# Expert mixture behind three attention layers: order of the last two experts, the last down product by column halves, the router's product with its columns held, the first weight remainders on GpSimd

## The reference

```python
def expert_choice_moe(h, w_router, w_gate, w_up, w_down):
    cap = CAPACITY_FACTOR * S // N_EXPERTS                    # 128
    aff = softmax(einsum('bsd,de->bse', h, w_router), axis=-1)
    g, idx = lax.top_k(aff.transpose(0, 2, 1), cap)
    xin = hb[ib]                                              # gather, for each expert
    a = einsum('becd,edf->becf', xin, w_gate)
    u = einsum('becd,edf->becf', xin, w_up)
    y = einsum('becf,efd->becd', silu(a) * u, w_down)
    y = y * g[..., None]
    return zeros((S, D)).at[ib].add(y)                        # scatter-add

    h2 = rmsnorm(x, norm_ffn_g) * (1.0 + sc2) + sh2           # in the block
    x = x + g2 * expert_choice_moe(h2, w_router, w_gate, w_up, w_down)
```

## Time and profile before

| | us |
|---|---|
| median of 3 runs | 2714.86 (2714.76 to 2715.02) |
| the profiled execution, timed | 2715.4 |
| its span | 2713.6 |
| window attention | 1836 to 2063 |
| router stage | 2063 to 2112.5 |
| experts | 2112.5 to 2713.6 |

### The profile page before, as it was taken

How to read it: one execution, slowest core, us unless ns; L and a number is a source line. 1 busy time by engine, 2 the same in 40 slices (tenths; PEclk the granted TensorE clock), 3 DMA queues, 4 the chain that set the end, 5 groups by cost and what they waited for, 6 DMA issues and landing times. The chain is left out here.

```text
span 2713.6 us, 32074 instructions
## 1 busy us (share of the span) xinstructions
PE 2501.0 (92%) x11641; PEld 1627.9 (60%) x11641; DVE 1729.4 (64%) x3267; ACT 1253.3 (46%) x2017; POOL 505.4 (19%) x525
## 2 busy tenths in 40 slices
PE   7999999699998899989999997999994699999997
PEld 3344444354555886446556656885552588888886
DVE  2799999677764421325654436506556688888885
ACT  2221110254554266345455542244444477777773
POOL 0000001011110000008677640000220011111111
PEclk9999999899999899999999997998996799999999
DMA  3011831211010332045343224030014799999994
GB/s 132 8 62 38 75 93 39 89 40 48 24 46 17 134 94 68 12 145 159 112 120 110 82 78 142 4 126 32 32 47 170 280 377 385 388 383 387 391 388 158
DMA packets 123818, 374.19 MB, mean 138 GB/s; under 512 B 22552, under 2 KB 31464, under 8 KB 122128
## 3 DMA queue, kind: packets, MB, share of 16 engines
q1 hardware_dynamic: 106064, 312.34, 31.3%
q0 software_dynamic: 17600, 59.81, 9.6%
HBM read 327.00 MB, written 45.11 MB: 137 GB/s over the span
## 5 line engine op out<-in xcount | busy, mean ns | idle before, releaser
L513 PE MATMUL ps<-l_hT,l_w 128*128 128x512 f32 (+1 forms) x832 | 364.3, 597 | 2.6 <-DVE l_hT L242 2.6
L513 PEld LDWEIGHTS ps<-l_hT,l_w 128*128 128x128 f32 (+1 forms) x832 | 155.3, 189 | 204.3 <-issue 204.2
L964 ACT ACTIVATE a_pT<-ps 128x512 f32<-128x512 f32 (+3 forms) x368 | 164.1, 487 | 173.6 <-PE ps L850 172.8
L894 PE MATMUL ps<-l_wo,a_mixT 128*128 128x512 f32 x384 | 182.1, 602 | 3.3 <-ACT l_klT L988 1.1
L1505 DVE MAX8 l_best<-sel 128x8 f32<-128x384 f32 (+5 forms) x192 | 171.6, 894 | 5.4
L976 ACT ACTIVATE a_p<-ps,a_stat 128x384 f32<-128x384 f32 (+7 forms) x192 | 129.2, 673 | 88.8 <-DVE a_stat L1050 49.9
L1506 DVE MATCH_REPLACE8 sel<-l_best,sel 128x384 f32<-128x384 f32 (+5 forms) x192 | 168.1, 876 | 0.0
L976 ACT ACTIVATE l_lat<-ps,a_stat 128x1024 f32<-128x1024 f32 (+7 forms) x128 | 94.8, 741 | 150.0 <-DVE a_stat L1050 149.1
L835 PE MATMUL ps<-l_kT,l_raw 96*128 96x512 f32 (+3 forms) x384 | 147.3, 492 | 5.7 <-ACT l_lat L976 4.1
L850 PE MATMUL ps<-ident,a_p 128*128 128x128 f32 x608 | 97.9, 290 | 30.8 <-DVE a_p L1063 27.5
L2737 POOL DMA_INDIRECT out_dram<-m_q,e_token x16 | 39.6, 2478 | 463.1 <-DVE m_q L2905 463.1
(11 more groups left out here) (460 smaller groups left out, 5712.5 us busy)
## 6 DMA issues: line engine op xcount, KB each, us to landing
x_raw<-in_w_gate SPq DMA_DIRECT2D x25, 2048.0 KB, 11.1
x_raw<-in_w_up SPq DMA_DIRECT2D x24, 2048.0 KB, 11.4
x_raw<-in_w_down SPq DMA_DIRECT2D x23, 2048.0 KB, 10.1
ada_w<-in_w_ada POOLq DMA_DIRECT2D x64, 384.0 KB, 3.7
m_ufT<-in_w_down SPq DMA_DIRECT2D x9, 2048.0 KB, 12.0
m_ufT<-in_w_up SPq DMA_DIRECT2D x8, 2048.0 KB, 11.7
l_w<-in_e_w_in SPq DMA_DIRECT2D x7, 2048.0 KB, 8.5
m_ufT<-in_w_gate SPq DMA_DIRECT2D x7, 2048.0 KB, 9.9
```

Source lines behind the costliest of these rows:

```text
L513: last = nc.tensor.matmul(self.t.ps[0:m, bank, :], w[:, c, col * P:col * P + m], hT[:, c, half * 512:(half + 1) * 512], start=c == 0, stop ...
L894: last = nc.tensor.matmul(t.ps[:, 7, :], self.lhs_out(n, self.order[n], c), self.w_out[:, c, h * 512:(h + 1) * 512], start=c == 0, stop=c ...
L964: self.k.nc.scalar.activation(dst, src, ACT.Copy).then_inc(self.moved["act"], 1)
```

## The change

Four edits.

1. In the window attention the router's columns become the stationary operand: `wg` is widened to 32 columns, of which 16 are zero, and chunk `c` of a block goes to the column group `c % 4`, that is to 32 rows of PSUM. ACT copies the four partial sums (`r_part`), and one more matmul with a matrix `pick` of ones adds them and turns them back, at the first pair of the next block (`sum_parts`). Blocks 6 and 7 are done as before.
2. The remainders of the first three halves are made on GpSimd in the router stage, between its stores and its gather, instead of on DVE at the start of the experts.
3. At the end up(15) runs ahead of down(14); the loads, ACT's and DVE's lists follow, h(15) is transposed within down(14) and goes to the buffer of `x_T0`.
4. Down(15) is made in column halves: 24 matmuls for columns 0 to 511, then 24 for the others. Each half has its own scaling and its own indirect DMA, with row numbers `halves` for an output seen as 2048 rows of 512.

```diff
+        elif b >= 0 and u % at.per == self.TURN + 1:
+            x = at.turns[u, "part"]
+            old = at.in_order[x.n - 2]
+            e.wait_ge(at.moved[old.engine], old.moved)
+            e.wait_ge(at.moved["act"], at.turns[u - 1, "row", 1].moved)
+            for i in range(2):
+                for g in range(4):
+                    c = 4 * i + g
+                    last = self.nc.tensor.matmul(self.t.ps[32 * g:32 * g + 32, x.bank, 0:P], self.wg[:, c, :], self.rT[b % 2][:, c, :],
+                                                 start=i == 0, stop=i == 1)
+            last.then_inc(at.turned, 1)
+
+    def sum_parts(self, e, at, b):
+        col = self.COL + EXPERTS * self.place(b)
+        e.wait_ge(at.moved["act"], at.turns[at.per * (b + 2) + self.TURN + 1, "part"].moved)
+        self.nc.tensor.matmul(self.t.ps[:, 6, col:col + EXPERTS], self.parts[b % 2][:], self.pick[:], start=True, stop=True).then_inc(self.routed, 1)
 
     def pe_beside(self, e, at, u):
 
-        b = u // at.per - 2
-        if b >= 0 and u % at.per == self.TURN + 1:
-            e.wait_ge(at.moved["act"], at.turns[u - 1, "row", 1].moved)
-            self.logits(b, range(KD))
+        b = u // at.per - 3
+        if b >= 0 and u % at.per == 0:
+            self.sum_parts(e, at, b)
...
         if m == self.UP:
-            return 6 * x + 2
+            return 6 * x + 2 if x + 1 < EXPERTS else 6 * x
...
-        return 6 * x + 6 if x + 1 < EXPERTS else 6 * x + 4
+        return 6 * x + {EXPERTS - 2: 8, EXPERTS - 1: 4}.get(x, 6)
...
+            for n in range(weights.SLOTS):
+                weights.low(e, n, nc.gpsimd)
             e.wait_ge(x_out, 16 * NB)
             e.wait_ge(told, 1)
             gather(0)
...
-            e.wait_ge(scattered, 16 * EXPERTS)
+            e.wait_ge(placed, 3)
+            for i in range(2):
+                e.wait_ge(yready, EXPERTS + i)
+                e.wait_ge(scattered, 16 * LAST)
+                nc.gpsimd.indirect_dma_start(t.out.rearrange("s (i d) -> (s i) d", i=2), bass.IndirectOffsetOnAxis(ap=halves[:, i:i + 1], axis=0),
+                                             last_y[:, 512 * i:512 * i + 512], None, compute_op=ALU.add).then_inc(scattered, 16)
+            e.wait_ge(scattered, 16 * (EXPERTS + 1))
...
+            for x in range(LAST):
+                up(x)
+                gate(x + 1, x)
+                if x == LAST - 1:
+                    up(LAST)
+                down(x)
+            last_down()
...
-            weights.low(e, 0)
-            weights.low(e, 1)
             e.wait_ge(xturn, 2)
...
-            for n in range(2, 5):
+            for n in range(SLOTS, 5):
                 weights.low(e, n)
```

More of the change, by code:

```diff
@@ L790, in __init__ @@
                     n += 1
+            elif rows and u >= 2 * self.per and u % self.per == rows.TURN + 1:
+                moved["act"] += 1
+                before = [x.used for x in self.turns.values() if x.n == n - 4]
+                self.turns[u, "part"] = Turn(n, "act", moved["act"], None, before[0])
+                n += 1
             ready += pair.joined
@@ L1174, in __init__ @@
         self.nc, self.t, self.a, self.gain, self.y = k.nc, t, a, gain, y
-        self.wr, self.wg = k.sb("r_w", [P, KD, EXPERTS]), k.sb("r_wg", [P, KD, EXPERTS])
+        self.wr, self.wg = k.sb("r_w", [P, KD, EXPERTS]), k.sb("r_wg", [P, KD, 32])
+        self.parts = [k.sb(f"r_part{i}", [P, P]) for i in range(2)]
+        self.pick = k.sb("r_pick", [P, EXPERTS])
         self.shift = k.sb("r_shift", [P, KD, P])
@@ L1268, in act @@
             if b >= 2:
-                e.wait_ge(self.routed, b - 1)
+                e.wait_ge(at.turned, at.turns[u - 2 * at.per + 1, "part"].n + 1)
             for i in range(2):
@@ L1274, in act @@
             self.square(e, b).then_inc(self.squared, 1)
+        elif b >= 0 and u % at.per == self.TURN + 1:
+            x = at.turns[u, "part"]
+            e.wait_ge(at.turned, x.n + 1)
+            if b >= 2:
+                e.wait_ge(self.routed, b - 1)
+            self.nc.scalar.activation(self.parts[b % 2][:], self.t.ps[:, x.bank, 0:P], ACT.Copy).then_inc(at.moved["act"], 1)
     def act_end(self, e, at):
-        e.wait_ge(self.routed, NB - 3)
+        e.wait_ge(at.turned, at.turns[len(at.pairs) - 1, "part"].n + 1)
         for i in range(2):
@@ L2564, in high, with low @@
                                       self.raw[n % self.RAWS].rearrange("p k n -> p (k n)"), ACT.Copy).then_inc(self.high_made, 1)
-    def low(self, e, n):
+    def low(self, e, n, engine=None):
         if n < self.N:
@@ L2570, in low @@
             high, rest = (x[:].rearrange("p k n -> p (k n)") for x in self.w[i])
-            self.nc.vector.tensor_tensor(rest, self.raw[n % self.RAWS].rearrange("p k n -> p (k n)"), high.bitcast(F32),
-                                         ALU.subtract).then_inc(self.split, 1)
+            (engine or self.nc.vector).tensor_tensor(rest, self.raw[n % self.RAWS].rearrange("p k n -> p (k n)"), high.bitcast(F32),
+                                                     ALU.subtract).then_inc(self.split, 1)
 def router_stage(k, a, t, keep, at, gate_w, token, weights, gather):
@@ L2728, in _ @@
         def _(e):
-            for x in range(EXPERTS):
+            for x in range(LAST):
                 for n in (1, 2) if x == 0 else (x + 2,):
@@ L2784, in gate, with up @@
                         chunk(x, xT[x % 2], GATE, 0, i, c)
-            turn_x(0)
-            gate(0)
-            for x in range(EXPERTS):
+            def up(x):
                 if x:
@@ L2796, in _, with down @@
                         turn_x(1)
-                if x < LAST:
-                    gate(x + 1, x)
-                else:
-                    turn_h(x)
+            def down(x):
                 if x:
@@ L2809, in _, with last_down @@
                         turn_x(x + 2)
+                        if x == LAST - 1:
+                            turn_h(LAST)
+            def last_down():
+                n = weights.at(LAST, DOWN)
+                e.wait_ge(silu, LAST + 1)
+                for half in range(2):
+                    cols = slice(half * 512, (half + 1) * 512)
+                    for i in range(2):
+                        e.wait_ge(w_split, n + i + 1)
+                        e.wait_ge(hsplit, 2 * LAST + i + 1)
+                        high, low = w[(n + i) % SLOTS]
+                        for c in range(HK):
+                            for j, (l, r) in enumerate(((last_hT[0], high), (last_hT[0], low), (last_hT[1], high))):
+                                last = nc.tensor.matmul(ps[:, half, :], l[:, i * HK + c, :], r[:, c, cols],
+                                                        start=i + c + j == 0, stop=i == 1 and c == HK - 1 and j == 2)
+                    last.then_inc(last_made, 1)
+            turn_x(0)
+            gate(0)
+            for x in range(LAST):
+                up(x)
+                gate(x + 1, x)
+                if x == LAST - 1:
+                    up(LAST)
+                down(x)
+            last_down()
         @block.scalar
@@ L2844, in _, with high_h @@
             first_of_h(0)
-            for x in range(EXPERTS):
+            def high_h(x, dst):
+                for i in range(2):
+                    e.wait_ge(hturn, 2 * x + i + 1)
+                    nc.scalar.activation(flat(dst[0][:, 4 * i:4 * i + 4, :]), ps[:, 2 + i, :], ACT.Copy).then_inc(hhigh, 1)
+            for x in range(LAST):
                 weights.high(e, 6 * x + 5)
@@ L2849, in _ @@
                 weights.high(e, 6 * x + 6)
-                for i in range(2):
-                    e.wait_ge(hturn, 2 * x + i + 1)
-                    if x:
-                        e.wait_ge(w_used, done(x - 1, DOWN))
-                    nc.scalar.activation(flat(hT[0][:, 4 * i:4 * i + 4, :]), ps[:, 2 + i, :], ACT.Copy).then_inc(hhigh, 1)
+                if x:
+                    e.wait_ge(w_used, done(x - 1, DOWN))
+                high_h(x, hT)
                 weights.high(e, 6 * x + 7)
@@ L2860, in _ @@
                 weights.high(e, 6 * x + 10)
+            high_h(LAST, last_hT)
+            weights.high(e, weights.N - 1)
         @block.vector
@@ L2881, in _, with result_h @@
                                         ALU.subtract).then_inc(xready, 1)
-            for n in range(2, 5):
+            for n in range(SLOTS, 5):
                 weights.low(e, n)
-            for x in range(EXPERTS):
-                weights.low(e, 6 * x + 5)
-                if x == 0:
-                    low_x(1)
+            def result_h(x):
                 e.wait_ge(silu, x + 1)
@@ L2890, in _, with low_h @@
                 nc.vector.tensor_tensor(h[:], h[:], ps[:, 2:4, :].rearrange("p a n -> p (a n)"), ALU.mult).then_inc(hready, 1)
-                weights.low(e, 6 * x + 6)
+            def low_h(x, dst):
                 for i in range(2):
```

50 lines of the change are left out of this document (41 added, 9 removed).

## The result

| | us |
|---|---|
| before, median of 6 runs | 2714.94 (2711.55 to 2717.71) |
| after, median of 6 runs | 2696.3 (2692.78 to 2698.82) |
| ratio | 0.9929, 95% interval 0.9917 to 0.9942 |
| forecast | 2696.4, range 2692.5 to 2705.5 |
| the profiled execution of after, timed / span | 2692.78 / 2691.0 |

The change takes 18.6 us off. The profiled execution of after is the fastest of its six, so the two spans are 22.6 us apart, 4 more than the medians. Stretches of the two traces are therefore compared from one event to another, never by their place in the span.

What follows compares the result with a forecast made beforehand. It took PE to bound the window attention and middle experts, DVE's subtractions the experts' start, and PE's waits and scatters the end. Gains 4 + 6.5 + 8 = 18.5 us gave 2696.4 against the median, range 2692.5 to 2705.5.

Steps and rivals of the forecast that it cites:

- Part 1: Window attention: router's columns stationary in four column groups, blocks 0 to 5, 4 us less, bounds +1.9 and -6.3.
- the columns do not overlap: Rival in window attention: the router product in column groups costs 1.9 us instead of giving 4, 2702.3; chance 8%.
- Part 2: Start of the experts: first three remainders on GpSimd, gate(0) starts at 2116.7 instead of 2123.26, 6.5 us less.
- given back: Rival at the experts' start: late transfers or slower GpSimd leave 0 instead of 6.5 us, 2702.9; chance 12%.
- Part 3: Experts' end: up(15) ahead of down(14), last down and scatter in column halves, 8 us less, bounds -3.6 and -9.
- The port: Slower rival in the router stage: DVE's top-k locks out with GpSimd's subtractions, up to 26.4 us, 2722.8; chance 7%.

Runs made afterwards that it cites:

- run 1: Before with only the router edit (columns stationary in four column groups, plus a summing product): 2709.8 us, 0.998 against before.
- Run 5: After, with all eight router products of a block summed in one column group instead of four: 2704.1 us.
- run 7: After, with 20 unused matmuls added to keep PE busy ahead of gate(0): 2695.9 us in a single run.
- run 2: Before with only the first three remainders moved to GpSimd: 2706.6 us, 0.9962 against before.
- run 3: Before with only the experts' end changed (up(15) ahead of down(14), last down by column halves): 2707.6 us, 0.9969 against before.
- run 4: After, with the last down whole again, in the old order with one scatter of 1024 columns: 2694.3 us, 0.9926 against before.
- Run 8: After, with one small unused DVE add, both inputs in SBUF, in each of the 16 top-k rounds: 2721.3 us.
- run 9: After, last down by weight halves, expert 14 scaled before the last remainder, which awaits scatter 14's issue and is made in two column halves: 2693.7 us.

## Why the prediction was right

**Part 1, -4.** Right in kind, and undersized. The four-group record was the one term without a row; I assumed 0.05 us, it is 0.036, nearly the 0.028 of a full overlap. The sum of the parts costs 0.14 a block and not 0.21. Per block 0.99 instead of 0.7, in all 5.9 by the rows, 5.8 by the stretch of the two profiles, 5.1 by the medians of run 1. The waits that I costed at nothing were 0.3 us once. Run 5 shows the rival "the columns do not overlap" as it would have been: 2704.1 for my 2702.3.

The Trainium skill (TensorEngine Tiling (Array Packing), Theoretical Speedup) has up to 4x for this shape; the runs show 1.87 / 0.57 = 3.3 between one group and four, the switch back to the full array within the 0.57.

**Part 2, -6.5.** Right term by term: 8.85 us apiece for the 8.8 taken from the earlier trace rows, the last over at 2096.2 with 3.9 us to the gather, gate(0) 2.1 us behind the transposes' end, the 3.2 us wait for `x_T1l` still there. The landings had 0.7 and 1.2 us of slack for the 0.5 and 1.0 forecast, so the rival "given back" was about as near as I thought. What I left out is PE's clock behind its idle stretch: gate(0)'s 48 matmuls took between 12.8 and 13.8 us in the traces of ten kernels (before, after and all but run 7), in no order that the edits explain. So one profile tells the gain no better than to a microsecond or so. Up to the transposes of h(0) it is 6.9 us between before and after, 6.4 between before and run 2; the other 1.1 us of the 8.0 in the table lie in the steady part behind (493.2 us in before and in run 2, 492.0 in after), which the change does not touch.

**Part 3, -8.** 7.1 in the stretch. PE ends 6.3 us earlier relative to the multiplication of h(14), for 6.2 forecast; its wait is 0.7 and not 1.2. Scatter 14 landed in 6.10 us, as summed. The term that was missized is what follows: between that landing and the next issue I had nothing, the chain shows 0.78 us (2679.99 to 2680.77), so the last scatter is issued 1.5 us behind PE's end and not 1.0. And the half scatter's end: 8.4 us from its issue to the span's end for my 5.0 + 3.0 = 8.0. Together 0.9 us, the whole difference between forecast and this profile; but the stretch of the same end varies by 1.0 us (run 3), so only the 0.78 us is sure, which stands between landing and issue in all six kernels whose last scatters wait for scatter 14 (0.77 to 0.78). The range from issue to the span's end is 7.9 to 8.4 us for the last half scatter, and the 8.0 that I summed lies in it. One thing that I counted as a gain is none, the column halves: the shorter vector instruction and the shorter landing stood in the sum with 0.6 and 1.1 us, and run 4 has the same time without them.

**The port.** Against it I had only one row of another instruction (L1027 in the earlier trace rows) and gave 7%. Run 8 bears out both halves: an instruction that meets the lock waits for the rest of GpSimd's, and the top-k's instructions don't meet it.

**The sum.** 4 + 6.5 + 8 = 18.5 stood for 18.6 by the medians; the stretches say 5.8 + 6.6 + 7.1 = 19.5. The errors of parts 1 and 3, +1.8 and -0.9, cancelled by half, and the medians are uncertain by some 3 us, so that the total came within 0.1 us is chance. The lower end of the range is 0.4 us off its own sum: 2714.9 - 22 is 2692.9, not 2692.5, which changes nothing.

## What to carry to other kernels

A small operand made stationary paid here only with its products in different column groups side by side; exchanged alone it lost. Work moved to an idle GpSimd was free beside a top-k that streams one input from SBUF, and a DVE instruction with two such inputs paid the rest of GpSimd's instruction, however small it was: count the inputs, not the sizes. The same holds for an indirect DMA that GpSimd issues beside such an instruction. At the end of a kernel follow the scatters as a queue of their own, with the issue, the landing and the 0.8 us from a landing to the next issue, before splitting the last one: here the split was worth nothing while the scatter ahead of it was in the way, and with that out of the way no run parts its worth from the rest.

## What the runs showed of the hardware

- A scatter's issue on GpSimd took 1.55 to 1.57 us with DVE idle or working from PSUM, and 5.50 and 5.57 us beside DVE's subtraction of two operands in SBUF (4.4 us long); with the subtraction held back it took 1.57 again (run 9). So the exclusion that run 8 shows from GpSimd's side, 8.26 us for an add of 0.16, has a counterpart: DVE's two-input instructions hold up GpSimd's preparation of a DMA.
- This is no matter of the end alone. 30 of the 32 indirect DMAs of the experts in before, and all but five or fewer in every other trace, are issued beside such a subtraction. In all 11 traces the issue then ends 1.44 to 1.52 us behind the subtraction for a scatter and 0.80 to 0.88 us for a gather (undisturbed a gather's issue takes 0.96 to 1.05). GpSimd's and DVE's timelines of before:

```profile
2216.93 2.33 POOL L2737 DMA_INDIRECT out_dram<-m_q,e_token  x1 [28.47 <-DVE m_q L2905]
2219.56 4.16 POOL L2510 DMA_INDIRECT m_q<-xn_d,e_token  x1 [0.30 <-issue]
...
2216.57 1.22 DVE L2867 TENSOR_TENSOR x_T1l<-m_q,x_T1h 128x1024 fp32r<-128x1024 f32 x1
2218.43 4.42 DVE L2571 TENSOR_TENSOR x_w1l<-x_raw,x_w1h 128x4096 fp32r<-128x4096 f32 x1 [0.65 <-ACT x_w1h L2563]
```

  The scatter's issue ends at 2219.26, 1.47 us behind the first subtraction (2217.79), the gather's at 2223.72, 0.87 behind the second (2222.85). DVE isn't held in turn: its second subtraction begins within the scatter's issue and takes its usual 4.42 us.
- After PE had stood still, with a granted clock of 0.50 in the 20 us ahead of the transposes, gate(0)'s first matmuls in after came at about half pace: 0.85 us from one pair to the next, later 0.47. The granted clock from 2105 to 2123 is 0.74. With 20 idle matmuls ahead (run 7) it was 1.00, and gate(0) ran its 48 in 11.3 us.
- 16 float32 records of 128 moving columns took 0.57 us in four column groups of 32, and 1.87 us in one.
- From the last scatter's issue to the span's end it took 7.9 to 8.4 us in the seven traces where it writes 512 columns, and 9.1 to 9.2 in the four where it writes 1024. In all seven another half scatter was issued 1.9 to 2.3 us ahead of it, so the two groups differ in more than the size.
